# A fused network of twelve sublayers: MLA's latents taken first, softmax normalised by diagonal matrices, and a third of MLA's modulation columns moved to VectorE

## The reference

```python
cond = jax.nn.silu(c)
mod = (cond @ w_mod[i] + b_mod[i]).reshape(-1, N_SUBLAYERS, N_MOD, D_MODEL)

def _sublayer(x, fn, mod_j, g, b, weight):
    shift, scale, gate = mod_j[:, 0, None, :], mod_j[:, 1, None, :], mod_j[:, 2, None, :]
    y = fn(x * (1 + scale) + shift)
    return _layernorm(DEEPNORM_ALPHA * x + weight * gate * y, g, b)
```

```python
# MLA
q = (_rmsnorm(cq, q_norm_g) @ w_q_up)
kv = (_rmsnorm(ckv, kv_norm_g) @ w_kv_up)
sc = jnp.einsum('bqhd,bkhd->bhqk', qb, kb) * scale
p = jax.nn.softmax(jnp.where(mask, sc, -jnp.inf), axis=-1)
o = jnp.einsum('bhqk,bkhv->bqhv', p, vb)
# differential
sc = jnp.einsum('bqhid,bkhid->bhiqk', qb, kb) * scale
p = jax.nn.softmax(jnp.where(mask, sc, -jnp.inf), axis=-1)
a = (p[:, :, 0] - lam * p[:, :, 1])
o = jnp.einsum('bhqk,bkhe->bqhe', a, vb)
```

## Time and profile before

| | us |
|---|---|
| median of three runs | 3048.01 (3044.29 to 3054.64) |
| the profiled execution | 3059.89, its span 3058.1 |
| TensorE busy | 2769.6 (91% of the span) |
| VectorE busy | 1963.1 (64%) |
| ScalarE busy | 1248.5 (41%) |
| GpSimd busy | 1449.5 (47%) |
| DMA | 573.20 MB read, mean 188 GB/s |

### The profile page before, as it was taken

The page is one execution under the profiler, slowest core; times in us unless marked ns, Lnnn a source line. Parts: engine busy times, 40 slices in busy tenths (PEclk is TensorE's granted clock), DMA queues, the critical chain, the costliest instruction groups (busy, mean ns, idle before and its releaser), DMA issues.

```text
span 3058.1 us, 49684 instructions
## 1 busy us (share of the span) xinstructions
PE 2769.6 (91%) x20691; PEld 2623.7 (86%) x20691; DVE 1963.1 (64%) x2277; ACT 1248.5 (41%) x1386; POOL 1449.5 (47%) x1134
## 2 busy tenths in 40 slices
PE   3998789999984999999989899999878999879999
PEld 3997689999983899999974899899768998679998
DVE  6656866576558765756676675765776555684654
ACT  2434444444433444444442443444434433344443
POOL 0890949659385396692970089298190000000000
PEclk7998889999996999999985899999889998889999
DMA  7775557667562576674740377486553643234453
GB/s 272 258 257 160 178 167 268 233 202 259 193 224 86 181 264 222 216 261 170 263 159 1 131 233 260 157 280 232 166 181 128 223 167 124 70 97 138 152 178 124
DMA packets 357446, 576.23 MB, mean 188 GB/s; under 512 B 22271, under 2 KB 297914, under 8 KB 357178
## 3 DMA queue, kind: packets, MB, share of 16 engines
q1 hardware_dynamic: 357306, 574.29, 55.6%
HBM read 573.20 MB, written 1.05 MB: 188 GB/s over the span
## 4 chain that ended last, share of the span: by engine, by line
PE 72%; DVE 12%; POOL 7%; ACT 3%; issue 3%; DMA 2%; SPq 1%; POOLq 0%; DVEq 0%; ACTq 0%
PE ps L1771 59%; POOL mod_acc L657 4%; PE ps L1824 3%; DVE wlo L1084 2%; POOL mod_w L652 2%; PE ps L2154 2%; ACT whi L695 1%; PE ps L1830 1%; PE ps L2145 1%; PE ps L1881 1%; DMA raw<-in_ffn_w_in_dram 1%; DVE z L1237 1%; DVE z L1215 1%; DMA mod_w<-in_w_mod_dram 1%; DVE conv L1514 1%
## 5 line engine op out<-in xcount | busy, mean ns | idle before, releaser
L1084 DVE TENSOR_TENSOR wlo<-raw,whi 128x2048 fp32r<-128x2048 f32 x387 | 982.4, 2541 | 620.7 <-ACT whi L695 618.9
L1771 PE MATMUL ps<-H_hi,whi 128*128 128x256 f32 x3840 | 1099.7, 286 | 47.1 <-issue 17.5
L1771 PE MATMUL ps<-H_lo,whi 128*128 128x256 f32 x3840 | 1093.5, 285 | 0.0
L1771 PE MATMUL ps<-H_hi,wlo 128*128 128x256 f32 x3840 | 1093.1, 285 | 0.0
L695 ACT ACTIVATE whi<-raw 128x2048 fp32r<-128x2048 f32 (+1 forms) x402 | 760.0, 1892 | 648.8 <-DMA raw<-in_ffn_w_in_dram 259.6
L1771 PEld LDWEIGHTS ps<-H_hi,whi 128*128 128x128 f32 x3840 | 744.3, 194 | 55.6 <-issue 45.8
L657 POOL TENSOR_TENSOR mod_acc<-mod_acc,mod_w 128x512 f32<-128x512 f32 x450 | 790.4, 1784 | 0.0
L1771 PEld LDWEIGHTS ps<-H_lo,whi 128*128 128x128 f32 x3840 | 744.5, 194 | 1.2 <-issue 1.0
L1771 PEld LDWEIGHTS ps<-H_hi,wlo 128*128 128x128 f32 x3840 | 744.2, 194 | 0.0
L1771 PE MATMUL ps<-A_hi,whi 128*128 (+1 forms) x1880 | 537.1, 286 | 21.5 <-DVE wlo L1084 21.5
L1771 PE MATMUL ps<-A_hi,wlo 128*128 (+1 forms) x1880 | 534.6, 284 | 0.0
(11 more groups left out here) (339 smaller groups left out, 2931.7 us busy)
## 6 DMA issues: line engine op xcount, KB each, us to landing
raw<-in_ffn_w_in_dram SPq DMA_DIRECT2D x176, 1024.0 KB, 5.3
mod_w<-in_w_mod_dram SPq DMA_DIRECT2D x180, 768.0 KB, 5.0
raw<-in_ffn_w_out_dram SPq DMA_DIRECT2D x88, 1024.0 KB, 5.0
raw<-in_w_gate_up_dram SPq DMA_DIRECT2D x22, 1024.0 KB, 5.1
raw<-in_ssm_w_in_dram SPq DMA_DIRECT2D x20, 1024.0 KB, 7.3
raw<-in_w_in_dram SPq DMA_DIRECT2D x14, 1024.0 KB, 5.1
raw<-in_diff_w_in_dram SPq DMA_DIRECT2D x12, 1024.0 KB, 8.1
raw<-in_w_down_dram SPq DMA_DIRECT2D x11, 1024.0 KB, 4.9
```

Of the source, the lines that this page charges most:

```text
L1084: tt(wlo[b % RAW][:, r], raw[b % RAW][:, r], whi[b % RAW][:, r].bitcast(F32), ALU.subtract).then_inc(w_lo, 1)
L1771: m = pe.matmul(out, l, r, start=first and i == 0, stop=last and i == 2, skip_group_check=rest)
```

## The change

1. In MLA, VectorE takes the first latent's `latent_n`, the convert of `kv.b` and `latent_lo` ahead of the two modulation units of k = 0 and the carry. ScalarE converts `kv.b` ahead of the second latent. The latents use `std[:, 0]` alone, since the carry now comes later and reads `std[:, 1]`.
2. In MLA, for k of 2 and more, GpSimd takes columns 0 to 1024 of a unit, VectorE the last 512 (`modulate_side`): twelve sides, two behind the converts of the queries, three in the query loop, seven in heads 0 to 6. SP's next load of a half waits for both. The converts of `q.b + 4` and `q.b + 5` move into heads 1 and 3.
3. In mla, diff and xatt the queries are scaled by the negative of the scale as they leave PSUM. VectorE takes the minima straight from PSUM (L1422), ScalarE's exp reads PSUM with a scale of −1, and the causal mask is added by TensorE (L2040), an fp32r matmul of the unit matrix with the negated mask. The scores of head h+2 wait for the exp of head h. The inverse sums (L1433) go onto diagonal matrices that ScalarE writes (`scales`: two copies of 128x128 a head, four in diff), and the transpose is an fp32 matmul of `prob` with the diagonal (L2055), which for diff adds both maps. The dilated attention stays as it was.
4. In `ln`, the opening block is rounded on ScalarE at c = 2 instead of 4 and on VectorE after `sqsum(1)` instead of `sqsum(3)`. The last norm (`ln_last`) keeps its order.

The core of the diff:

```diff
+SIDE = 2 * PIECE
+def side_count(sub, k):
+    return (sub - 2) // 9 * (DC - MLA_DVE) + k + 1 - MLA_DVE
+def split_unit(sub, k):
+    return sub in (2, 11) and k >= MLA_DVE
...
                 sp.wait_ge(mod_used[half], DC * sub + k)
+                of = (sub, k - 1) if k else (sub - 1, DC - 1)
+                if split_unit(*of):
+                    sp.wait_ge(mod_side[half], side_count(*of))
...
-                pieces = [slice(i, i + PIECE) for i in range(0, MODU, PIECE)]
+                pieces = [slice(i, i + PIECE) for i in range(0, SIDE if split_unit(sub, k) else MODU, PIECE)]
...
+                def scales(h):
+                    act.wait_ge(s["summed"], n["summed"] + h + 1)
+                    for x in range(2 * maps):
+                        i = nc.scalar.activation(diag[:, h % 2, x, :], ident if x < 2 else lam_ident[:, :], ACT.Copy,
+                                                 scale=stat[:, h % 4, 12 + x:13 + x])
+                    i.then_inc(s["probs"], 1)
...
-                    if c == 4:
+                    if c == (2 if st.kind == "ln" else 4):
                         convert(g.b + g.n + 1)
...
                 convert(kv.b - 1)
                 latent_std(0, KVR)
+                convert(kv.b)
                 latent(1, 2)
                 latent_hi(0, 0, 2)
-                convert(kv.b)
...
+            def modulate_side(sub, k, half):
+                dve.wait_ge(mod_loaded[half], 16 * (DC * (sub - 1) + k + 1))
+                if k == MLA_DVE:
+                    dve.wait_ge(mod_used[half], DC * sub + k)
+                else:
+                    dve.wait_ge(mod_side[half], side_count(sub, k) - 1)
+                r = slice(SIDE, MODU)
+                stt(mod_acc[:, half, r], mod_w[:, half, r], cond[:, k:k + 1], mod_acc[:, half, r], ALU.mult, ALU.add).then_inc(mod_side[half], 1)
...
                 gated(0), gated(1), zsum(1), sqsum(1)
+                if st.kind == "ln":
+                    convert_open(st, 0)
                 gated(2), gated(3), zsum(2), zsum(3), sqsum(2), sqsum(3)
-                convert_open(st, 0)
+                if st.kind == "ln_last":
+                    convert_open(st, 0)
...
+                        first = score_bank(h, 0, maps)
+                        for t, (x, y) in enumerate(tiles):
+                            top = stat[:, b, 0:2 * maps].rearrange("p (m t) -> p t m", m=maps)[:, t, :]
+                            i = nc.vector.tensor_reduce(top, ps[:, first:first + maps, x:y], AX, ALU.min)
+                        i.then_inc(s["maxed"], 1)
...
+                def attended(h):
+                    if h in (1, 3):
+                        convert(q.b + 4 + h // 2)
+                    if h < 7:
+                        modulate_side(sub, 4 + (h + 1) // 2, (h + 1) % 2)
...
                 convert(kv.b - 1)
+                latent_n(0, 0, 2)
+                convert(kv.b)
+                latent_lo(0, 0, 2)
                 modulate(sub, 0, 0)
                 modulate(sub, 0, 1)
                 carry(st)
-                latent_n(0, 0, 2)
-                latent_lo(0, 0, 2)
-                convert(kv.b)
...
+                        seen = "maxed" if kind == "dilated" else "exped"
+                        pe.wait_ge(s[seen], n[seen] + h - 1)
...
+                            if causal:
+                                m = pe.matmul(ps[:, b, o + keys - P:o + keys], unit[:, :], mask[:, :], start=False, stop=True,
+                                              skip_group_check=True)
...
+                        for x in range(maps):
+                            m = pe.matmul(ps[:, turned_bank(h), b:b + P], prob[:, h % 4, x * CW + a:x * CW + a + P], diag[:, h % 2, 2 * x + t, :],
+                                          start=x == 0, stop=x == maps - 1)
```

More of the change, by code:

```diff
@@ L160, in column @@
         o += r
-ATT = ("scores", "maxed", "exped", "probs", "turned", "turned_out", "mixed", "mixed_out")
+ATT = ("scores", "maxed", "exped", "summed", "probs", "turned", "turned_out", "mixed", "mixed_out")
 SIGNALS = {
@@ L404, in program @@
         pick = at("pick", [P, 11], room(44), F32R)
+        unit, mask = at("unit", [P, P], room(4 * P), F32R), at("mask", [P, P], room(4 * P), F32R)
+        lam_ident = at("lam_ident", [P, P], room(4 * P))
         std = at("std", [P, 2, S], room(8 * S))
@@ L751, in attend @@
                         exps(i)
+                    if 1 <= i <= heads and kind != "dilated":
+                        scales(i - 1)
                     if 2 <= i < heads + 2:
@@ L766, in act_init @@
                 nc.scalar.activation(tiny[:, 6:8], tiny[:, 4:6], ACT.Exp).then_inc(s["lam_exp"], 1)
+                copy(unit[:, :], ident)
+                nc.scalar.activation(mask[:, :], kc("causal", 0, P), ACT.Copy, scale=-1.0)
                 copy(pick[:, :], kc("pick")).then_inc(s["picked"], 1)
@@ L895, in act_mla, with linear_evac @@
                 projected(st)
-            def linear_evac(g, dst, func=ACT.Copy, start=0, count=None):
+            def linear_evac(g, dst, func=ACT.Copy, start=0, count=None, scale=lambda j: 1.0):
                 for j in range(start, count or g.n):
@@ L1344, in projected, with attend @@
                         tt(mod_lo[:, :, :], mod_acc[:, :, :], mod_hi[st.kind][:, :, :].bitcast(F32), ALU.subtract).then_inc(s["mod_lo"], 1)
-            def attend(n, heads, scale, kind):
+            def attend(n, heads, scale, kind, after=lambda h: None):
                 maps = 2 if kind == "diff" else 1
@@ L1380, in normal @@
                             link(i)
-                    link(nc.vector.reciprocal(stat[:, b, 12:12 + 2 * maps], stat[:, b, 8:8 + 2 * maps]))
-                    if kind == "diff":
-                        link(ts(stat[:, b, 14:16], stat[:, b, 14:16], tiny[:, 0:1], None, ALU.mult))
+                    inverse = nc.vector.reciprocal(stat[:, b, 12:12 + 2 * maps], stat[:, b, 8:8 + 2 * maps])
+                    if kind != "dilated":
+                        inverse.then_inc(s["summed"], 1)
+                        return
+                    link(inverse)
                     for t, (x, y) in enumerate(tiles):
                         i = ts(prob[:, b, x:y], prob[:, b, x:y], stat[:, b, 12 + t:13 + t], None, ALU.mult)
-                    if kind == "diff":
-                        link(i)
-                        for t, (x, y) in enumerate(tiles):
-                            i = stt(prob[:, b, x:y], prob[:, b, CW + x:CW + y], stat[:, b, 14 + t:15 + t], prob[:, b, x:y],
-                                    ALU.mult, ALU.add)
                     i.then_inc(s["probs"], 1)
@@ L1412, in attend @@
                         maxima(i)
+                        after(i)
                     if 1 <= i <= heads:
@@ L1951, in attend @@
                 full = kind == "xatt"
+                causal = kind in ("mla", "diff")
+                maps = 2 if kind == "diff" else 1
                 def parts(h):
```

72 lines of the change are left out of this document (42 added, 30 removed).

## The result

The changed kernel takes 3038.51 us (median of 19 runs, 3029.39 to 3046.39) where the one before takes 3057.2 (19 runs). The ratio is 0.9942 with a 95% interval of 0.9931 to 0.9953: faster by 18 us, not by the 45 forecast, and its time lies above the forecast's 3030. The profiled executions differ by 21.4 us of span. From here on I set the two traces side by side at the same places of the program (TensorE's first product of each modulation row, and of each norm's statistics), and give what each stretch contributed.

What follows compares the result with a forecast made beforehand. TensorE carried 72% of the waits, VectorE 12%, GpSimd 7%; in the MLA and differential attentions TensorE wasn't the bound. −24 (MLA) −15 (differential) +1.8 (cross attention) −8 (norms) = −45, from 3048 to 3003 us; range 2983 to 3030.

Steps and rivals of the forecast that it cites:

- norms: Nine norms outside MLA: early rounding of the opening block gives −0.9 us each, −8 in all.
- tails: MLA's projection and norm: 29.5 us instead of 36.6 and 34.4, −7.1 and −4.9.
- cross attention: Cross attention: fp32 turns cost about .45 us more a head than transposes, +1.8 for four.
- The head's pace is about 4.25: MLA's attention: mod loads limit a head to about 4.25 us instead of 5.1; attention 39 us, −2 and −4.
- second rival: MLA: sides queue behind loads and maxima behind sides, units stretch from 4.0 toward 5.9; 3027 us, chance .09.
- all of MLA's 24 us: Both MLAs together: latents, attention and tails, −24 us, bounds −34 and −10.
- The scores go from 0.93 to MLA's 1.3, then 0.3 for four masks: Differential mixer, TensorE: a head's scores take 1.3 us and masks 0.3, within 3.6 a head at 2.4 GHz.
- −15: Differential attention: heads at 4.3 us instead of 6.5, over seven heads −15 us, bounds −22 and +5.
- The low clock: Differential heads stay at 1.2 GHz, 7.2 us instead of 4.3 in seven heads: +20, 3023 us, chance .09.
- The latents' 3.1 us each: MLA: reordered latents fill VectorE's idle times, its chain to the first query block 3.1 us shorter in each MLA.
- third rival: Norms: early rounding holds up the mod row, +1 instead of −0.9 for every norm; +17, 3020 us, chance .04.
- The signs of being wrong: Wrong if heads stay above 5 us in both mixers, or if mod row copies begin later than now.

Runs made afterwards that it cites:

- m_nosides: Changed kernel with GpSimd doing all columns of MLA's modulation units and VectorE no sides; ratio 0.9912 to the kernel before.
- m_convback: Changed kernel with the two converts of heads 1 and 3 back in MLA's query loop; ratio 0.9917 to the kernel before.
- m_sides5: Changed kernel with five of MLA's seven attention sides in heads 0, 2, 4, 6, 7 and two behind the attention; ratio 0.985 to the kernel before.
- d_grouped: Changed kernel with a differential head's four masks behind all its scores; output not the reference's, read for time alone; ratio 0.9872 to the kernel before.
- d_pairs: Changed kernel with the differential mixer's masks in pairs, after both maps' scores for a query block; ratio 0.9884 to the kernel before.
- d_dvemask: Changed kernel with VectorE adding the differential mixer's mask on the way from PSUM to `prob`, diagonals kept; ratio 0.9894 to the kernel before.
- x_transposes: Changed kernel with the cross attention normalised on VectorE and turned by transposes again; ratio 0.9933 to the kernel before.
- lat_old: Changed kernel with MLA's latents behind the two modulation units and the carry again; ratio 0.9948 to the kernel before.
- l_oldorder: Changed kernel with the opening block rounded at its old place in the eleven `ln` norms; ratio 0.9967 to the kernel before.

## Why the prediction was wrong

Direction, norms, tails and cross attention came out as their terms had it. Two terms failed, and with them 27 of the 45 us. Of the 35 us between the forecast 3003 and the measured 3038.5, another 9 come from the base: the median of before was 3048 over three runs and is 3057.2 over 19.

**"The head's pace is about 4.25", attention 39 us (−2, −4, and the −3.1 each of the queries before it).** Where nothing disturbed them, a side took 0.78 us (1.3 taken), GpSimd's unit the 4.0 forecast, and a round of one half's buffer 8.8 (355.6 to 364.4; 8.4 forecast). What failed is the step from a rate to an end. I put seven sides from the start of the attention on, as if their loads were waiting there, and gave no price to the roundings that the change itself puts into heads 1 and 3. The chain of mod loads has a start of its own: GpSimd's first tick is at 304.1, and its twelve units end at 373.3, 5.8 us each, because roundings and rotations on VectorE beside it stretch three of the units to 6.9 or more (the second took from 309.4 to 317.1), and because an early load had to wait for side (2, 0), which VectorE reached at 313.2. The sides tied the attention to the end of that chain. `m_nosides` (33.4 us), `m_convback` (a start 4.3 us later, the same end) and `m_sides5` (8.9 and 13.0 us won back without leaving out any work) show it. This was my second rival, "sides set the pace", in its mechanism; I priced it as the loss of all of MLA's 24 us, and it took only the 12 of queries and attention. The units did stretch to 5.8 us on average, as the rival had it, but more by the roundings than by the sides.

**"The scores go from 0.93 to MLA's 1.3, then 0.3 for four masks".** They went to 3.0 at full clock and 5.3 at the low one. I took the masks' price from MLA's rows, where all products have 128 rows; where products of 64 rows stand around them each mask costs some 0.5 us instead of 0.1. `d_grouped` and `d_pairs` show that by moving them alone. `d_dvemask`, with the masks back on VectorE, shows that the rest was sized rightly: without the masks on TensorE the attention is 13.4 us shorter than before (56.8 to 43.4), where the forecast had −15. The low clock was the rival for this term. It was there (0.51 for 27 us with TensorE busy throughout, against 0.87 over the whole in `d_grouped`). The two can be told apart in part. `x_transposes` ran the changed kernel's differential attention in 52.0 us at a clock of 0.81, `d_pairs` took 41.7 at 0.80: at the same clock the masks' place costs 10 us. And in the trace of the changed kernel a head takes 5.15 us at full clock and 8.0 at the low one. By my estimate from these, seven heads at 5.15 would have been 9.5 us shorter than before instead of 15: about 6 us of the miss are the masks' at full clock, the other 9.5 came with the low clock. Whether the masks bring the low clock about is open.

**The latents' 3.1 us each** were read from true idle times, and they do come back at the rotation of the keys (3.0 and 2.7 in `lat_old`). But they don't carry through to the first score, and from norm to norm `lat_old` shows 1.5 and −0.5, inside the spread: an idle on a chain whose end is set elsewhere. The first score of the first MLA came 7 us earlier mostly by the two converts that moved out of the query loop, to which I had given no term, and by the 2.1 us at the end of the norm.

**The tails** were 29.5 forecast and 30.3 measured, with the steps in the order given. The 0.8 us are the opening block's rounding, earlier in these norms too, where it delays the mod row: with the old order (`l_oldorder`) the tails took 29.3 and 29.2. It is the third rival, in the two norms that I had left out of the term. The two MLAs as a whole weren't shorter there, since their attentions ended later.

**The signs of being wrong.** The heads did stay above 5 us in both mixers: 48.4/8 = 6.0 in MLA, 5.15 at full clock in the differential one. The copies of the mod row did begin later, 4.3 to 5.1 us after the row's first product instead of 3.0 in the nine norms. This last was no bad sign: those norms became 0.9 us shorter all the same.

That the profiled execution of before was 11.9 us above the median of three runs was for the most part those runs' luck: it is 2.7 above the median of 19.

## What to carry to other kernels

A piece of work put into another engine's queue as a filler brings its waits with it: before placing it, lay the time at which its data arrive beside the time at which its place in the queue comes up, over the whole chain, not at its steady rate. Here moving two of seven short instructions behind the attention, and sparing two heads one, was worth more than the whole change.

The price of a matrix product is that of its neighbours too. Where small products of 64 rows run side by side, put 128-row ones in groups behind them and not between them (3.0 us a head here against 1.6 and 1.7).

## What the runs showed of the hardware

- A 128-row fp32r product of 128 columns between 64-row fp32 ones costs about 0.5 us at full clock, and 0.17 in a group of four behind them (0.66 for four).
- TensorE can be busy without a gap and stay at the lower clock: 27.39 of 27.40 us at 0.51, with 64-row scores, masks between them and, from 923 on, the turns of two heads. From 934.6 on, with the same mix in shorter turns, the clock was 0.94. The Trainium skill, *TensorE: Matmul & The Clock Gate*, "Part 4: PE-mode transpose", has it that transposes don't count as busy in the same way; there is none in this stretch of the changed kernel, so they are not the reason here. By that page the low rate had seemed the less likely, and it came all the same.
- GpSimd's products beside a two-input operation of VectorE's (348.79 and 349.87) took 3.92 us instead of 1.36: 2.56 more, where the operation lasts 2.27.
